# Norms after the two feed-forwards: statistics by token from the sums' banks, the residual added there by TensorE, normed pieces turned back

## The chip, the cores and the metric

The kernel runs on one core of one Trainium2 chip. The metric is the device time of one execution in microseconds (us); three runs of the kernel before are given. PE is TensorE, PEld its weight loads, DVE is VectorE, ACT is ScalarE, POOL is GpSimd and SP is SyncE, which here only issues DMAs.

## The reference

The model is two blocks of two layers each on 256 tokens of width 1024, in float32. The change touches only the second block, and in it only the residual and layer norm behind each feed-forward:

```
DEEPNORM_ALPHA = (2 * DEPTH) ** 0.25        # DEPTH = 2
def layer_norm(x, g, b):
    mu = jnp.mean(xf, -1, keepdims=True)
    var = jnp.mean(jnp.square(xf - mu), -1, keepdims=True)
    y = (xf - mu) * lax.rsqrt(var + LN_EPS) * g + b
def conv_ffn(x, w_up, conv_w, conv_b, w_down):        # w_up 1024 x 5632, w_down 2816 x 1024
    h = causal_depthwise_conv(x @ w_up, conv_w) + conv_b
    gate, val = jnp.split(h, 2, axis=-1)
    return (jax.nn.silu(gate) * val) @ w_down
for layer in range(DEPTH):                            # the second block
    mix = even_mixer(...) if layer % 2 == 0 else odd_mixer(...)
    h = layer_norm(DEEPNORM_ALPHA * h + mix, ln_g[layer, 0], ln_b[layer, 0])
    ffn = conv_ffn(h, ...)
    h = layer_norm(DEEPNORM_ALPHA * h + ffn, ln_g[layer, 1], ln_b[layer, 1])
return h
```

## The kernel before

The running activation `X` lies in SBUF by feature: 128 partitions hold 128 features, and eight chunks of 256 columns hold the tokens. Weights stream as 842 tiles of 128x1024 through a ring of four slots (SP, L447). Every product of the large weights is made in three passes of split float32: ACT writes the high part of each half tile (`split_high`, L1200), DVE the low part (`split_low`, L2241), and PE multiplies low by high, high by low and high by high (L537 to L539, or L579 to L581). Each engine has its own program, written out by hand in the order of issue; semaphores order the engines against each other. The `h_high` and `h_low` operands of a product are the split of its input, made in pairs of chunks (L1309, L1913, L1917), and a product's first tile waits for each pair.

`conv_ffn` first makes the 44 chunks of the up projection (`split_linear`), with the convolution and the gate on ACT and DVE. Then `down` runs 22 tiles: `split_sums` holds a pair of token blocks of the gated activation still and streams the weight rows, so that the sums lie by token in the four banks of `PA`: bank `t * 2 + b` has token block `t` (128 tokens) and features `512 b` to `512 b + 511`. A filler matmul (`busy`, L601) stands between the up and the down part, and others in the norms.

Behind the last down tile comes this chain. ACT and DVE copy `PA` to `TMP` (L1270, L1848; `TMP` is a part of `BIG`, and that name stands in the rows). PE turns 16 blocks of 128x128 back to features in `PB` (`turn_sums`, L589). DVE adds the residual chunk by chunk (`add_chunk`, L1841). PE sums `X` over the features with a matrix of 1/1024 (L642), DVE subtracts the mean (L1936), ACT squares (L1261), PE sums the squares (L628), ACT takes the root (L1265), DVE its reciprocal on 128x256 (L1893) and scales (L1898), and ACT applies gain and shift (`affine`, L1303). After the first feed-forward the odd mixer's product `odd_in` follows, and between its first and its second tile eight small gate matmuls (L1094). After the second, SP stores the four pairs of `X` (L482).

## Time and profile before

| | us |
|---|---|
| median of 3 runs (lowest to highest) | 3028.68 (3025.34 to 3029.73) |
| profiled execution, its own time | 3028.78 |
| its span from first to last instruction | 3027.1 |
| PE busy in it | 2913.8 (96%) |
| DVE busy | 2272.9 (75%) |
| ACT busy | 1646.3 (54%) |

The profiled execution lies 0.10 us above the median, and 1.68 us of its time lie outside the span. A busy PE is not a PE at its peak: matmuls overlap, so one that takes 0.40 us starts 0.23 us after the one ahead of it. The mean granted clock of TensorE was 0.991 of full.

### The profile page before, as it was taken

The page shows a single profiled execution, that of the slowest core. Times are in us where ns is not written, and L with a number is a line of the kernel's source. Part 1 is how long each engine was busy: PE and PEld are TensorE (multiplying, and loading weights), DVE is VectorE, ACT ScalarE, POOL GpSimd, SP SyncE. Part 2 cuts the span into 40 slices and gives each one's busy share as a digit, 9 for nine tenths or more (in the row PEclk, how much of TensorE's full clock was granted, in tenths as well). Part 3 has the DMA queues.
Part 4 walks back from the last instruction along what each step waited for, and adds up shares of the span by engine and source line. Part 5 has one row for each costly group of instructions (what it writes and reads, how often), then busy time and mean ns, then how long its engine had stood idle before and what let it go on. Part 6 is the DMA issues. An engine that isn't in the chain of part 4 may idle for free.

```text
span 3027.1 us, 58260 instructions
## 1 busy us (share of the span) xinstructions
PE 2913.8 (96%) x19784; PEld 2655.7 (88%) x19784; DVE 2272.9 (75%) x4828; ACT 1646.3 (54%) x3387; POOL 62.0 (2%) x112
## 2 busy tenths in 40 slices
PE   7988999999999999999999999999999999999998
PEld 6988999999887778899999988888898889797896
DVE  5586598888779984759888877777585678765786
ACT  2323557778544443655777854444554258463574
POOL 2000000000001100000000000000000000000000
PEclk9999999999999999999999999999999999999999
DMA  9611454444478853445444455555442155432453
GB/s 367 260 54 63 167 186 158 154 161 140 165 265 307 309 194 119 139 167 186 157 153 161 140 173 187 187 188 188 142 140 70 43 172 173 160 126 84 152 175 118
DMA packets 137688, 503.07 MB, mean 166 GB/s; under 512 B 15312, under 2 KB 15440, under 8 KB 137264
## 3 DMA queue, kind: packets, MB, share of 16 engines
q1 hardware_dynamic: 122544, 445.63, 43.5%
q0 software_dynamic: 14976, 55.19, 5.1%
q8 instruction: 107, 1.75, 0.2%
q14 instruction: 61, 0.50, 0.1%
HBM read 498.65 MB, written 2.10 MB: 165 GB/s over the span
## 4 chain that ended last, share of the span: by engine, by line
PE 82%; DVE 6%; ACT 3%; issue 2%; DVEq 0%; ACTq 0%
PE PB L537 14%; PE PB L538 14%; PE PB L539 13%; PE PA L580 9%; PE PA L581 9%; PE PA L579 9%; PE PA L773 4%; PE PB L527 2%; DVE w_low L2241 2%; PE PA L985 1%; DVE BIG L2267 1%; PE PA L1159 1%; PE PA L628 1%; ACT w_high L1200 1%; PE PB L985 1%
## 5 line engine op out<-in xcount | busy, mean ns | idle before, releaser
L1200 ACT ACTIVATE w_high<-ring 128x512 fp32r<-128x512 f32 x1596 | 992.1, 630 | 886.6 <-PE PA L581 466.3
L2241 DVE TENSOR_TENSOR w_low<-ring,w_high 128x512 fp32r<-128x512 f32 x1596 | 1084.2, 691 | 454.8 <-ACT w_high L1200 439.4
L537 PE MATMUL PB<-h_high,w_low 128*128 128x256 f32 x3984 | 1139.4, 286 | 20.7 <-DVE h_low L1917 10.5
L538 PE MATMUL PB<-h_low,w_high 128*128 128x256 f32 x3984 | 1124.6, 282 | 0.0
L539 PE MATMUL PB<-h_high,w_high 128*128 128x256 f32 x3984 | 1122.0, 282 | 0.0
L537 PEld LDWEIGHTS PB<-h_high,w_low 128*128 128x128 f32 x3984 | 760.3, 191 | 34.8 <-issue 17.1
L538 PEld LDWEIGHTS PB<-h_low,w_high 128*128 128x128 f32 x3984 | 753.9, 189 | 0.4 <-issue 0.2
L539 PEld LDWEIGHTS PB<-h_high,w_high 128*128 128x128 f32 x3984 | 753.2, 189 | 0.0
L579 PE MATMUL PA<-w_low,a_high 128*128 128x512 f32 x1200 | 470.4, 392 | 7.8 <-DVE a_low L2250 7.0
L580 PE MATMUL PA<-w_high,a_low 128*128 128x512 f32 x1200 | 476.3, 397 | 0.0
L581 PE MATMUL PA<-w_high,a_high 128*128 128x512 f32 x1200 | 474.0, 395 | 0.0
L579 PEld LDWEIGHTS PA<-w_low,a_high 128*128 128x128 f32 x1200 | 225.4, 188 | 74.0 <-DVE a_low L2250 9.8
L580 PEld LDWEIGHTS PA<-w_high,a_low 128*128 128x128 f32 x1200 | 224.9, 187 | 53.0
L581 PEld LDWEIGHTS PA<-w_high,a_high 128*128 128x128 f32 x1200 | 225.2, 188 | 49.3
L773 PE MATMUL PA<-onehot_b,onehot_a 128*128 128x128 f32 x1024 | 137.6, 277 | 2.9 <-issue 2.6
L2250 DVE TENSOR_TENSOR a_low<-BIG,a_high 128x256 fp32r<-128x256 f32 x300 | 127.6, 425 | 10.3
L773 PEld LDWEIGHTS PA<-onehot_b,onehot_a 128*128 128x128 f32 x1024 | 124.8, 191 | 6.7 <-issue 3.3
L1860 DVE SCALAR_TENSOR_TENSOR BIG<-BIG,coef 128x1024 f32<-128x1024 f32 (+1 forms) x80 | 102.5, 1281 | 13.6 <-DMA BIG<-ada 12.3
L1414 ACT ACTIVATE onehot_a<-inv,slots 128x128 f32<-128x128 f32 x256 | 111.0, 481 | 0.0
L2267 DVE SCALAR_TENSOR_TENSOR BIG<-PB,par,BIG 128x255 f32 (+3 forms) x176 | 84.5, 480 | 14.8 <-DVE BIG L2267 14.5
L1409 ACT ACTIVATE inv<-con,slots 128x128 f32<-128x128 f32 x256 | 88.5, 393 | 4.8 <-PE PA L773 3.2
L2181 DVE TENSOR_TENSOR onehot_b<-con,slots 128x512 f32<-128x512 f32 x128 | 87.7, 685 | 0.0
(341 smaller groups left out, 2604.6 us busy)
## 6 DMA issues: line engine op xcount, KB each, us to landing
ring<-tiles SPq DMA_DIRECT2D x842, 512.0 KB, 3.3
BIG<-ada POOLq DMA_DIRECT2D x96, 512.0 KB, 6.9
BIG<-skew POOLq DMA_DIRECT2D x4, 512.0 KB, 4.5
X<-x SPq DMA_DIRECT2D x1, 1024.0 KB, 5.8
skew<-BIG POOLq DMA_DIRECT2D x1, 1024.0 KB, 6.6
out<-X SPq DMA_DIRECT2D x4, 256.0 KB, 2.1
con<-consts SPq DMA_DIRECT2D x1, 911.0 KB, 8.7
BIG<-masks POOLq DMA_DIRECT2D x1, 768.0 KB, 7.9
```

Source lines behind the costliest of these rows:

```text
L537: mm(dst, lhs_l, high, start=start, stop=False, skip_group_check=True)
L538: mm(dst, lhs_h, low, start=False, stop=False, skip_group_check=True)
L539: return mm(dst, lhs_h, high, start=False, stop=stop, skip_group_check=True)
L579: mm(dst, high[:, own], w_l, start=first, stop=False, skip_group_check=True)
L580: mm(dst, low[:, own], w_h, start=False, stop=False, skip_group_check=True)
L581: ins = mm(dst, high[:, own], w_h, start=False, stop=last, skip_group_check=True)
L773: ins = mm(PA[:, (g % 4 * 4 + i) * P:(g % 4 * 4 + i + 1) * P], onehot_a[:, i * P:(i + 1) * P], onehot_b[:, i * P:(i + 1) * P], start=True, ...
L1200: fn(tile_half(w_high, s, b), ring[:, at:at + HALF], ACT.Identity).then_inc(sem("high_ready"), 1)
L1414: ins = fn(onehot_a[:, i * P:(i + 1) * P], inv[:, i * P:(i + 1) * P], ACT.Relu, scale=slots[:, 3 * T + tok:3 * T + tok + 1], bias=slots[:, ...
L2241: tt(tile_half(w_low, s, b), ring[:, at:at + HALF], tile_half(w_high, s, b).bitcast(F32), ALU.subtract).then_inc(sem("low_ready"), 1)
L2250: tt(pair(a_low, j), a, pair(a_high, j).bitcast(F32), ALU.subtract)\
L2267: stt(dst, product_slot(q0 + j)[:, 0:T - sh], wt[tap][:, bass.ds(it * 4 + j, 1)], dst, ALU.mult, ALU.add).then_inc((taken, sem("conv_step" ...
```

## The change

The down sums no longer start from zero. `add_residual` first writes alpha times `X` into the four banks of `PA`, by token: 16 float32 matmuls that hold a 128x128 block of `X` still and stream a new constant, alpha times the identity; the filler between up and down goes. After the last down tile the layer norm is taken by token: DVE's `bn_stats` reads each bank as soon as its last matmul is done, `bn_aggr` makes mean and variance of each token, ACT takes two roots of one column, DVE makes a scale and a shift for each token. ACT then writes the normed first half of the features to `TMP`, DVE the second, PE turns the pieces back, and ACT applies gain and shift from `PB` straight into `X`. Two filler matmuls stand ahead of the turning. Three semaphores are merged into two names of the same kind (`exponent_ready`, `exponential_ready`), which moves nothing.

```diff
-    ("tri", P), ("strict", P), ("pairs", PAIR_LEVELS * P), ("eps", 2),
+    ("tri", P), ("strict", P), ("pairs", PAIR_LEVELS * P), ("eps", 2), ("alpha", P),
...
+        TOK_STATS, TOK_MEANS = inv[:, 0:TT * 12], inv[:, 24:24 + TT * 2]
+        TOK_ROOTS, TOK_SCALES, TOK_SHIFTS = inv[:, 28:28 + TT], inv[:, 30:30 + TT], inv[:, 32:32 + TT]
+        def token_piece(ap, t, b):
+            return ap[:, t * D + b * HALF:t * D + (b + 1) * HALF]
+        def turned(m):
+            at = (product_at["odd_in"][0] + m // 2) % 4 * 512 + m % 2 * T
+            return PB[:, at:at + T]
...
+            def add_residual():
+                for t in range(TT):
+                    for m in range(DC):
+                        mm(PA[:, t * D + m * P:t * D + (m + 1) * P], X[:, m * T + t * P:m * T + (t + 1) * P],
+                           c("alpha"), start=m % 4 == 0, stop=False, skip_group_check=True)
...
                         ins = mm(dst, high[:, own], w_h, start=False, stop=last, skip_group_check=True)
+                        if tokens and t == 0:
+                            ins.then_inc(sem("first_tokens"), 1)
...
+            def turn_normed():
+                for b, normed in enumerate(("sums_copied", "normed_by_dve")):
+                    for t in range(TT):
+                        pe.wait_ge(sem(normed), w.up(sem(normed)))
+                        for m in range(4 * b, 4 * b + 4):
+                            ins = nc.tensor.transpose(turned(m)[:, t * P:(t + 1) * P],
+                                                      TMP[:, t * D + m * P:t * D + (m + 1) * P], ident)
+                            if t and m % 2:
+                                ins.then_inc(sem("sums_turned"), 1)
...
                 def down(j, it=0):
-                    split_sums(c0 + j, s0 + 2 * FC + j, it, 4, j == 0, j == FC - 1)
-                busy(1, PA[:, 1024:1024 + HALF])
+                    split_sums(c0 + j, s0 + 2 * FC + j, it, 4, False, j == FC - 1, j == FC - 1)
+                add_residual()
...
-                turn_sums()
+                busy(2, PB[:, 0:HALF])
+                turn_normed()
...
+            def token_norm(name, run=None):                       # on ACT
+                if run is not None:
+                    split_high(run, 0)
+                for t in range(TT):
+                    act.wait_ge(sem("mean_ready"), w.up(sem("mean_ready")))
+                    fn(TOK_ROOTS[:, t:t + 1], TOK_MEANS[:, 2 * t + 1:2 * t + 2], ACT.Sqrt,
+                       bias=c("eps", 1, 1)).then_inc(sem("root_ready"), 1)
+                for t in range(TT):
+                    act.wait_ge(sem("scaled"), w.up(sem("scaled")))
+                    fn(token_piece(TMP, t, 0), token_piece(PA, t, 0), ACT.Identity, scale=TOK_SCALES[:, t:t + 1],
+                       bias=TOK_SHIFTS[:, t:t + 1]).then_inc(sem("sums_copied"), 1)
+            def turned_affine(i, name, run=None):
+                for m in range(DC):
+                    if m % 2 == 0:
+                        act.wait_ge(sem("sums_turned"), SUMS.index(name) * (DC // 2) + m // 2 + 1)
+                    ins = fn(X[:, m * T:(m + 1) * T], turned(m), ACT.Identity,
+                             scale=p("ln_g", i * DC + m, 1), bias=p("ln_b", i * DC + m, 1))
+                    if m % 2:
+                        ins.then_inc(sem("x_out"), 1)
+                        w.up(sem("x_out"))
+                        if run is not None and m // 2 >= HIGH_BY_ACT:
+                            act.wait_ge(sem("x_out"), (i + 1) * (DC // 2) + m // 2 + 1)
+                            fn(two(h_high, m // 2), two(X, m // 2), ACT.Identity).then_inc(sem("pair_high"), 1)
+                if run is not None:
+                    split_high(run, 1)
...
+            def token_norm(i, run=None):                          # on DVE
...
+                def scaled(t):
+                    dve.wait_ge(sem("root_ready"), w.up(sem("root_ready")))
+                    v.reciprocal(TOK_SCALES[:, t:t + 1], TOK_ROOTS[:, t:t + 1]).then_inc(done, 1)
+                    settled()
+                    stt(TOK_SHIFTS[:, t:t + 1], TOK_MEANS[:, 2 * t:2 * t + 1], -1.0, TOK_SCALES[:, t:t + 1],
+                        ALU.mult, ALU.mult).then_inc(sem("scaled"), 1)
+                def normed(t):
+                    dve.wait_ge(sem("scaled"), w.up(sem("scaled")))
+                    ts(token_piece(TMP, t, 1), token_piece(PA, t, 1), TOK_SCALES[:, t:t + 1],
+                       TOK_SHIFTS[:, t:t + 1], ALU.mult, ALU.add).then_inc(sem("normed_by_dve"), 1)
+                if run is not None:
+                    split_low(run, 0)
...
+                        v.bn_stats(TOK_STATS[:, at:at + 6], token_piece(PA, t, b)).then_inc(done, 1)
...
+                            v.bn_aggr(TOK_MEANS[:, 2 * t:2 * t + 2], TOK_STATS[:, t * 12:(t + 1) * 12])\
+                                .then_inc(sem("mean_ready"), 1)
...
+                for t in range(TT):
+                    scaled(t)
+                for t in range(TT):
+                    normed(t)
+                if run is not None:
+                    for m in range(DC // 2):
+                        split_fresh(X, "x_out", m)
+                    split_low(run, 1)
...
-        "eps": np.tile([1e-6, 1e-5], (P, 1)),
+        "eps": np.tile([1e-6, 1e-5], (P, 1)), "alpha": ALPHA * eye,
```

On PE, between the last up tile and the first down tile of each feed-forward, there stood before one filler matmul (L601):

```order
L539 MATMUL PB<-h_high,w_high 128x256
L183 REGISTER_ALU
L183 COMPARE_AND_BRANCH
L601 MATMUL PA<-con 128x512
L579 MATMUL PA<-w_low,a_high 128x512
```

Now 16 matmuls of `X` with the constant stand there (L585), and the first down tile (L597) is queued behind them:

```order
L550 MATMUL PB<-h_high,w_high 128x256
L183 REGISTER_ALU
L183 COMPARE_AND_BRANCH
L585 MATMUL PA<-con,X 128x128 x16
L597 MATMUL PA<-w_low,a_high 128x512
```

On DVE, behind the first feed-forward's last split of the gated activation, there stood before the copy of the sums, the residual, two tiles' low parts, the mean, the reciprocal of 256 columns and the scaling:

```order
L1848 COPY BIG<-PA 128x1024
L1841 SCALAR_TENSOR_TENSOR X<-X,PB 128x256 x8
L2241 TENSOR_TENSOR w_low<-ring,w_high 128x512 x2
L1936 TENSOR_TENSOR X<-X,PA 128x512 x4
L2241 TENSOR_TENSOR w_low<-ring,w_high 128x512 x2
L1893 RECIPROCAL inv<-inv 128x256
L1898 TENSOR_TENSOR X<-X,inv 128x512 x3
L1913 CAST h_high<-X 128x512
L1917 TENSOR_TENSOR h_low<-X,h_high 128x512
```

Now the low part of `odd_in`'s first tile comes ahead of the statistics, that of its second tile behind the split of `X`, and between them only four pieces of 512 columns are read from `PA` and two written:

```order
L2350 TENSOR_TENSOR w_low<-ring,w_high 128x512 x2
L2036 BN_STATS inv<-PA 128x6 x3
L2040 BN_AGGR inv<-inv 128x2
L2036 BN_STATS inv<-PA 128x6
L2040 BN_AGGR inv<-inv 128x2
L2015 RECIPROCAL inv<-inv 128x1
L2017 SCALAR_TENSOR_TENSOR inv<-inv 128x1
L2015 RECIPROCAL inv<-inv 128x1
L2017 SCALAR_TENSOR_TENSOR inv<-inv 128x1
L2022 TENSOR_SCALAR BIG<-PA,inv 128x512 x2
L1975 CAST h_high<-X 128x512
L1979 TENSOR_TENSOR h_low<-X,h_high 128x512
```

On ACT, behind the last feed-forward, there are now one table load, two roots of one column, two pieces and the eight chunks; the four squares and the copy of 1024 columns are gone:

```order
L1349 ACT_TABLE_LOAD
L1349 ACTIVATE inv<-inv,con 128x1 x2
L1353 ACTIVATE BIG<-PA,inv 128x512 x2
L1361 ACTIVATE X<-PB,par 128x256 x8
L207 UNCONDITIONAL_BRANCH
```

The table load stands ahead of the first root's wait and behind the last `split_high`, where it has nothing to wait for.

## Rows read from the trace of the kernel before

**Rows 1.** The page: shares of the chain that ended last, by engine

```profile
PE 82%; DVE 6%; ACT 3%; issue 2%; DVEq 0%; ACTq 0%
```

**Rows 2.** Stretches: length, busy (x count) of PE, PEld, DVE, ACT, POOL, PEclk, DMA, GB/s

```profile
2650.40:2655.90 5.50, 4.87 (x25) 4.66 (x26) 3.25 (x7) 2.86 (x6) 0.00 (x0) 0.69 0.00 0
...
2944.00:3005.50 61.50, 61.23 (x263) 48.85 (x261) 42.70 (x86) 25.29 (x40) 0.00 (x0) 1.00 0.43 146
3005.50:3024.60 19.10, 13.43 (x58) 9.52 (x58) 10.70 (x18) 9.22 (x15) 0.00 (x0) 0.99 0.08 29
```

**Rows 3.** Timeline behind the second feed-forward: start, duration, engine, line [idle before <-releaser]

```profile
3005.09 0.40 PE L581 MATMUL PA<-w_high,a_high 128*128 128x512 f32 x1
3005.53 1.23 DVE L1848 COPY BIG<-PA 128x1024 f32<-128x1024 f32 x1 [3.55 <-PE PA L581]
3006.80 1.97 PE L589 MATMUL PB<-con,BIG 128*128 128x128 f32 x16 [1.32 <-DVE BIG L1848]
3007.50 2.74 DVE L1841 SCALAR_TENSOR_TENSOR X<-X,PB 128x256 f32<-128x256 f32 x8 [0.75 <-PE PB L589]
...
3018.07 1.75 DVE L1893 RECIPROCAL inv<-inv 128x256 f32<-128x256 f32 x1 [3.26 <-ACT inv L1265]
...
3020.59 4.04 ACT L1303 ACTIVATE X<-X,par 128x256 f32<-128x256 f32 x8 [2.62 <-DVE X L1898]
...
3021.70 3.28 SPq L482 DMA_DIRECT2D out<-X  x4
```

**Rows 4.** Timeline around the first feed-forward's end and the odd mixer's start

```profile
2627.39 0.63 ACT L1200 ACTIVATE w_high<-ring 128x512 fp32r<-128x512 f32 x1 [0.76 <-PE PA L581]
...
2628.05 0.69 DVE L2241 TENSOR_TENSOR w_low<-ring,w_high 128x512 fp32r<-128x512 f32 x1 [0.70 <-ACT w_high L1200]
...
2632.53 0.40 PE L581 MATMUL PA<-w_high,a_high 128*128 128x512 f32 x1
...
2650.38 0.36 PE L537 MATMUL PB<-h_high,w_low 128*128 128x256 f32 x1 [1.26 <-DVE h_low L1917]
...
2652.38 0.41 PE L539 MATMUL PB<-h_high,w_high 128*128 128x256 f32 x1
...
2655.70 3.61 PE L1094 MATMUL PA<-X,SM 128*128 128x256 f32 x16
```

**Rows 5.** Timeline of PE between the first feed-forward's up and down parts

```profile
2568.17 1.02 PE L601 MATMUL PA<-con 128*128 128x512 f32 x2
...
2570.83 0.50 PE L579 MATMUL PA<-w_low,a_high 128*128 128x512 f32 x1 [1.64 <-DVE a_low L2250]
...
2573.49 0.40 PE L581 MATMUL PA<-w_high,a_high 128*128 128x512 f32 x1
...
2574.15 0.49 PE L579 MATMUL PA<-w_low,a_high 128*128 128x512 f32 x1 [0.26 <-DVE a_low L2250]
```

**Rows 6.** Groups by shape: count | busy us, mean ns of one | idle before

```profile
L1451 ACT ACTIVATE BIG<-PB,par 128x256 f32 x80 | 43.9, 548 | 0.0
L1614 ACT ACTIVATE BIG<-PB 128x256 f32<-128x256 f32 x24 | 9.2, 383 | 29.5 <-PE PB L539 29.5
L1261 ACT ACTIVATE BIG<-PA 128x512 f32<-128x512 f32 x6 | 3.6, 597 | 10.9 <-PE PA L732 10.9
L1791 DVE TENSOR_SCALAR BIG<-PB,par 128x256 f32<-128x256 f32 x8 | 4.4, 544 | 12.7 <-PE PB L527 12.7
```

**Rows 7.** Timeline: one-column steps and a reduction of 512 columns

```profile
2658.63 0.20 ACT L1619 ACTIVATE stat<-stat 128x2 f32<-128x2 f32 x1
...
2659.06 0.15 DVE L2534 TENSOR_SCALAR stat<-stat 128x1 f32<-128x1 f32 x1
...
2687.85 0.69 DVE L2508 TENSOR_REDUCE stat<-BIG 128x2 f32<-128x512 f32 x1
```

**Rows 8.** Timeline: 16 float32 matmuls of 128 columns in the first 40 us

```profile
22.38 3.65 PEld L616 LDWEIGHTS PB<-coef,BIG 128*128 128x128 f32 x32 [3.00 <-DMA BIG<-ada]
```

**Rows 9.** DMA issue of the constants: count, KB each, us from issue to landing

```profile
con<-consts SPq DMA_DIRECT2D x1, 911.0 KB, 8.7
```

More of the change, by code:

```diff
@@ L568, in split_linear, with split_sums @@
                 spans(pe, body, (first, n if last is None else last))
-            def split_sums(j, k, it, step, first=False, last=False):
+            def add_residual():
[3 more added lines that the diff above has]
+                           c("alpha"), start=m % 4 == 0, stop=False, skip_group_check=True)
+            def split_sums(j, k, it, step, first=False, last=False, tokens=False):
                 pe.wait_ge(sem("gated_ready"), it * 4 + (j + 1))
@@ L1617, in odd_mixer @@
                     if j == 0:
-                        act.wait_ge(sem("lam_sums"), w.up(sem("lam_sums")))
-                        fn(stat[:, 8:10], stat[:, 6:8], ACT.Exp).then_inc(sem("lam_exp"), 1)
+                        act.wait_ge(sem("exponent_ready"), w.up(sem("exponent_ready")))
+                        fn(stat[:, 8:10], stat[:, 6:8], ACT.Exp).then_inc(sem("exponential_ready"), 1)
                         act.wait_ge(sem("gate_psum"), w.up(sem("gate_psum")))
@@ L1654, in _ @@
             fn(coef[:, 0:DC], p("c", 0, DC), ACT.Silu).then_inc(sem("cond_ready"), 1)
-            act.wait_ge(sem("lb_shifted"), w.up(sem("lb_shifted")))
-            fn(coef[:, 40:48], coef[:, 40:48], ACT.Exp).then_inc(sem("lb_exp"), 1)
+            act.wait_ge(sem("exponent_ready"), w.up(sem("exponent_ready")))
+            fn(coef[:, 40:48], coef[:, 40:48], ACT.Exp).then_inc(sem("exponential_ready"), 1)
             act.wait_ge(sem("x_loaded"), w.up(sem("x_loaded"), 16))
@@ L1741, in _ @@
             conv_ffn(0)
-            layer_norm("down0", "odd_in")
-            norm_affine(1)
+            token_norm("down0", "odd_in")
+            turned_affine(1, "down0", "odd_in")
             odd_mixer()
@@ L1747, in _ @@
             conv_ffn(1)
-            layer_norm("down1")
-            norm_affine(3, split=False)
+            token_norm("down1")
+            turned_affine(3, "down1")
         @block.vector
@@ L1899, in scale @@
                         .then_inc(sem("scaled"), 1)
+                w.up(sem("scaled"), DC // 2)
                 if name is not None:
@@ L1942, in layer_norm, with settled @@
                 scale(X, "x_out" if run is not None else None)
+            def token_norm(i, run=None):
+                done = sem("dve_step")
+                def settled():
+                    dve.wait_ge(done, w.up(done))
+                def scaled(t):
[10 more added lines that the diff above has]
+                    split_low(run, 0)
+                r0, n = STREAM_AT[f"down{i}"]
+                s1 = SPLIT_AT[f"up{i}"][0] + 3 * FC
+                for b in range(2):
+                    for t in range(TT):
+                        if t == 0:
+                            dve.wait_ge(sem("first_tokens"), w.up(sem("first_tokens")))
+                        else:
+                            dve.wait_ge(*((sem("mid_tile"), s1), (tile_done, r0 + n))[b])
+                        at = (t * 2 + b) * 6
+                        v.bn_stats(TOK_STATS[:, at:at + 6], token_piece(PA, t, b)).then_inc(done, 1)
+                        w.up(done)
+                        if b:
+                            dve.wait_ge(done, w.value(done))
+                            v.bn_aggr(TOK_MEANS[:, 2 * t:2 * t + 2], TOK_STATS[:, t * 12:(t + 1) * 12])\
+                                .then_inc(sem("mean_ready"), 1)
+                            w.up(sem("mean_ready"))
+                            dve.wait_ge(sem("mean_ready"), w.value(sem("mean_ready")))
+                for t in range(TT):
+                    scaled(t)
+                for t in range(TT):
+                    normed(t)
[3 more added lines that the diff above has]
+                    split_low(run, 1)
             def inverse_heads(n):
@@ L2290, in conv_ffn @@
                 spans(dve, tile, (2, FC + 2, 2 * FC, 2 * FC + 2, 3 * FC))
-                add_sums(f"down{i}")
+                token_norm(i, ("odd_in", None)[i])
             def even_mixer():
@@ L2495, in odd_mixer @@
                 dve.wait_ge(sem("dve_step"), w.up(sem("dve_step")))
-                v.tensor_reduce(stat[:, 6:8], lv[:, :, 0, :], AX.X, ALU.add).then_inc(sem("lam_sums"), 1)
+                v.tensor_reduce(stat[:, 6:8], lv[:, :, 0, :], AX.X, ALU.add).then_inc(sem("exponent_ready"), 1)
                 def biased(n):
@@ L2700, in _ @@
             conv_ffn(0)
-            layer_norm(1, "down0", "odd_in")
             odd_mixer()
```

11 lines of the change are left out of this document (5 added, 6 removed).

## Prediction

> **What bounds the kernel now.** I read four views in this order. The page's chain of work that ended last puts 82% of the span on PE [rows 1], so a saving counts only where PE waits or where the last stage ends. The stretches then show two kinds of time: in the second down part PE is busy 61.23 us of 61.50 with 263 matmuls, one each 0.23 us, at the full granted clock, while behind it 19.10 us pass with DVE busy 10.70 and ACT 9.22: no engine is full, it is one chain [rows 2]. The timeline of that stretch shows it link by link, and the one at the first feed-forward and the one between up and down show the two other places that the change touches [rows 3 to 5].
>
> I call E the end of the last down matmul: 3005.09 + 0.40 = 3005.49 in the second feed-forward, 2632.53 + 0.40 = 2632.93 in the first [rows 3, 4]. Behind the second, the last chunk of `X` is ready at 3020.59 + 4.04 = 3024.63, so E + 19.14 [rows 3]. Behind the first, `odd_in` starts at 2650.38 = E + 17.45, and its first tile is followed by the gate matmuls at 2655.70 = E + 22.77 [rows 4]. From there PE goes on alone, so this second number is the one that passes to the end.
>
> **The change, part by part.**
>
> *Prices.* A reduction of 512 columns on DVE takes 0.69 us [rows 7], a copy of 1024 columns from PSUM 1.23 [rows 3], so 256 more columns cost (1.23 - 0.69) / 2 = 0.27. `bn_stats` stands nowhere in the trace. From below: it can't matter much under 0.69, since the first two banks are done before E. From above: the slowest row per column is the reciprocal, 1.75 us for 256 [rows 3], so 3.50 for 512. I take 0.69, the row of the same kind (one operand read once, a small result), and keep 1.4 (twice over the data) for the range. A one-column step costs 0.15 on DVE and 0.20 on ACT [rows 7], with 0.04 between steps. A piece of 512 from PSUM on ACT costs 0.60 plus two pointer operands; those cost 0.548 - 0.383 = 0.165 on 256 columns [rows 6], so 0.76. On DVE, 256 columns with two pointers take 0.544 [rows 6], 512 then 0.81. The eight chunks stay at 4.04 / 8 = 0.505 each [rows 3]; between 0.46 and 0.55 the tail moves by 0.4.
>
> *Behind the second feed-forward.* The four banks end at E - 2.09, - 1.39, - 0.70 and 0, three matmuls of 0.23 apart. DVE is free, so three `bn_stats` run from E - 2.05 to + 0.04, `bn_aggr` to 0.25, the fourth `bn_stats` 0.29 to 0.98, its `bn_aggr` to 1.17. The root of the second tokens ends on ACT at 1.41; meanwhile DVE makes the first tokens' scale and shift, ready at 1.6, and the second's at 2.0. ACT writes its pieces 1.62 to 2.4 and to 3.1, DVE 2.0 to 2.8 and to 3.65. The two fillers take PE to E + 2.0 at most (one takes 1.02 [rows 5]), ahead of the first piece. The turning of four blocks takes 4 x 0.12 (16 in 1.97), and the reader follows 0.45 behind the second block's start, as DVE's first add follows the fourth by about as much [rows 3]. The last pieces of the first features are turned from 3.15, so ACT's chunks start at 3.6. The second features are turned by 4.5, ahead of ACT. End: 3.6 + 4.04 = E + 7.65 against 19.14: **- 11.5 us**. The stores follow the chunks as before (issued over 3.28 us from the first pair on [rows 3]) and stay 2.5 us behind the last.
>
> *Behind the first feed-forward.* Here the low part of `odd_in`'s first tile is queued on DVE ahead of the statistics. Its second half needs the last but one down tile off PE (E - 2.79), then 0.63 on ACT and 0.69 on DVE [rows 4], so DVE is free at E - 1.37 and everything is 0.7 late against the other tail: chunks start at E + 4.35. The first pair is out at 5.4; DVE casts and subtracts it (0.42 and 0.69), and PE starts at E + 6.65 against 17.45. ACT does six chunks (to 7.4), a high part (0.63), two chunks, a high part (to 9.8), DVE the last low part to 10.5. A pair is six matmuls: 0.70 us at full clock. In the row at 2652.38 a matmul of 256 columns takes 0.41 instead of 0.28 and the stretch from 2650.40 has a granted clock of 0.69 [rows 2, 4]: part of the tile ran at 1.2 GHz, after gaps in PE's work. I take the same here: PE finishes pairs at 7.9, 9.2, 10.5 and 11.8. Gate matmuls at E + 11.8 against 22.77: **- 10.9 us**. The high part of the second tile has moved behind all this on ACT and its low part on DVE, ready by E + 12: the gate matmuls (3.6 us [rows 4]) cover it by 3 us, and with it the loads that SP issues on each low part. Without that cover it would cost up to 1.4.
>
> *Between up and down, twice.* 16 float32 matmuls of 128 columns took 3.65 us [rows 8]. They start at 2568.17, where the filler did, so the first down tile starts at 2571.83 instead of 2570.83: 1.0 late. It then ends at 2573.73 + 1.0, where the second tile started at 2574.15, held by the split of its activation on DVE [rows 5]: that slack of 0.4 is taken up, and **+ 0.6 each, + 1.2** goes on, since the down part is PE's alone. In the second feed-forward it is the same picture.
>
> *At the start.* The constants grow by 64 KB on 911, which landed in 8.7 us [rows 9], and all engines wait for them: 0 to + 0.6, I take **+ 0.3**. `bn` results, `TMP` and the merged semaphores cost nothing of their own.
>
> Sum against the profiled execution: 3028.78 - 11.5 - 10.9 + 1.2 + 0.3 = **3007.9**. The median of the runs is 0.1 lower than that execution; I say 3007.8.
>
> **A rule that speaks against it.** The rows show the granted clock at 0.99 through the stretch of [rows 2] that holds 16 turnings, fillers and sums; they don't show turnings with nothing dense behind them. The Trainium skill, "TensorE: Matmul & The Clock Gate", Part 4 (PE-mode transpose), says that the full clock "doesn't engage" for transposes. By that rule the turned pieces would not keep PE warm ahead of `odd_in`; the result would be the first rival below, by the row alone the sum above.
>
> **Rivals.**
> 1. *A cold start of the odd mixer.* Five fillers and sixteen summing matmuls stood ahead of `odd_in`; now only two fillers and the turnings, with gaps. If the slow level lasts through the tile and the gate matmuls, these take 7.2 instead of 3.6 us, less what the next tiles' ACT and DVE work hides. The slow stretch before was there at 2652.38 and gone at 2655.70, where 16 gate records take 3.61, so some 3 us [rows 4]; one that lasts through the gate matmuls too loses 1.5 to 3.6 more, I take 2.7: 3010.5. For it: PE idles from about E + 5 to 6.65, then 0.5 between pairs. Chance 0.22.
> 2. *`bn_stats` reads twice.* At 1.4 us the four of them end 0.7 x 4 = 2.8 later in each tail, since they stand one behind the other: 3007.8 + 5.6 = 3013.4. Against it: a reduction of 512 columns goes once over the data. Chance 0.10.
> 3. *The other side: `bn_stats` as slow per column as the reciprocal.* 3.50 each adds (3.50 - 0.69) x 4 = 11.2 per tail, 22.4 in all: 3030.2, slower than before. It decides from 3.3 us each. Nothing but that one row speaks for it. Chance 0.02.
> 4. *It is worth only one tail.* The odd mixer waits for something other than `X`, say its tables on POOL. Against: PE's first matmul there is released by `h_low` [rows 4]. 3007.8 + 10.9 = 3018.7, chance 0.02.
>
> **How the numbers follow.** The forecast has 0.64, the rivals the rest. The likeliest case has its own range of 3005.5 to 3010 (clock at full throughout - 0.6, chunks at 0.46 - 0.7, constants - 0.3; gaps of 0.1 on some ten links + 1 to 2). The range over the cases takes in rival 1 and most of rival 2: 3004.0 to 3013.5. What a measurement of this kernel can tell from no change is about 0.2%, 6 us; faster by more 0.96, within 0.02, slower 0.02.
>
> **What would show it.** In the changed kernel's timeline: `BN_STATS` at 0.69 us, three of them before E + 0.1; ACT's first chunk at E + 3.6 behind the second feed-forward and E + 4.35 behind the first; the last chunk's end at E + 7.65; the gate matmuls at E + 11.8; the 16 residual matmuls in 3.65 us and a second down tile that no longer waits. It would be wrong if a `BN_STATS` takes over 1.2 us, if the granted clock is low beyond `odd_in`'s first tile, or if ACT's chunks, and not PE or DVE, start later than the pieces allow.

## The result, and the profile after

| | before | after |
|---|---|---|
| median (lowest to highest), us | 3028.45 (3025.34 to 3029.73) | 3002.09 (3001.84 to 3006.80) |
| profiled execution, its span, us | 3028.78, 3027.1 | 3006.80, 3005.1 |
| time after by time before, all executions | | 0.9919, 95% interval 0.9906 to 0.9932 |

The change saves 26.4 us by the medians of four executions each. The forecast was 3007.8 with a range of 3004.0 to 3013.5, so the result is 1.9 us under the range. The profiled execution of the changed kernel took 3006.80, 22.0 less than the profiled one before, where the sum said 20.9. The other three took 3002.26, 3001.91 and 3001.84. Four executions are few: the interval of the ratio reaches up to 0.9932, and 0.9932 of 3028.45 is 3007.9, so this measurement misses the stated range and doesn't rule out the forecast's ratio of 0.9931 (3007.8 to 3028.68). So there are two questions: did the steps go as worked out, and where do 4.9 us between executions of one kernel come from?

The timeline of the changed kernel behind the second feed-forward answers to [rows 3]:

```profile
2993.09 2.09 DVE L2036 BATCH_NORM_STATS2 inv<-PA 128x6 f32<-128x512 f32 x3 [1.46 <-PE PA L599]
...
2994.74 0.40 PE L599 MATMUL PA<-w_high,a_high 128*128 128x512 f32 x1
...
2994.98 1.88 PE L632 MATMUL PB<-con 128*128 128x512 f32 x4
2995.21 0.21 DVE L2040 BATCH_NORM_AGGREGATE inv<-inv 128x2 f32<-128x12 f32 x1
...
2995.45 0.70 DVE L2036 BATCH_NORM_STATS2 inv<-PA 128x6 f32<-128x512 f32 x1
...
2996.43 0.29 ACT L1349 ACTIVATE inv<-inv,con 128x1 f32<-128x1 f32 x1 [0.68 <-DVE inv L2040]
...
2996.82 1.45 ACT L1353 ACTIVATE BIG<-PA,inv 128x512 f32<-128x512 f32 x2
...
2997.03 1.52 DVE L2022 TENSOR_SCALAR BIG<-PA,inv 128x512 f32<-128x512 f32 x2
...
2997.66 2.20 PE L610 MATMUL PB<-con,BIG 128*128 128x128 f32 x16 [0.80 <-ACT BIG L1353]
...
2998.80 3.76 ACT L1361 ACTIVATE X<-PB,par 128x256 f32<-128x256 f32 x8 [0.53 <-PE PB L610]
2999.85 3.07 SPq L493 DMA_DIRECT2D out<-X  x4
```

E is 2994.74 + 0.40 = 2995.14. The three first statistics end at 2995.18, E + 0.04. The chunks start at E + 3.66 and end at 3002.56, E + 7.42, where 19.14 stood before. One statistic takes 0.70, a piece 0.73 on ACT and 0.76 on DVE.

The same timeline behind the first feed-forward answers to [rows 4], and the first stretch below to [rows 2]; the second is one of the half-clock stretches in the odd mixer behind it (length, busy (x count) of PE, PEld, DVE, ACT, POOL, granted clock, DMA share, GB/s):

```profile
2632.76 0.39 PE L599 MATMUL PA<-w_high,a_high 128*128 128x512 f32 x1
...
2637.19 2.85 ACT L1361 ACTIVATE X<-PB,par 128x256 f32<-128x256 f32 x6 [0.53 <-PE PB L610]
...
2639.54 0.36 PE L548 MATMUL PB<-h_high,w_low 128*128 128x256 f32 x1 [1.30 <-DVE h_low L1979]
...
2639.74 0.28 PE L549 MATMUL PB<-h_low,w_high 128*128 128x256 f32 x1
...
2643.12 0.38 PE L548 MATMUL PB<-h_high,w_low 128*128 128x256 f32 x1 [0.54 <-DVE h_low L1979]
...
2643.94 3.62 PE L1126 MATMUL PA<-X,SM 128*128 128x256 f32 x16
```

```profile
2631.00:2645.00 14.00, 10.79 (x59) 7.94 (x58) 10.89 (x23) 10.28 (x21) 0.00 (x0) 1.00 0.16 59
2730.90:2737.70 6.80, 6.64 (x35) 4.72 (x36) 2.52 (x5) 0.01 (x1) 0.00 (x0) 0.50 0.01 1
```

E is 2632.76 + 0.39 = 2633.15, the chunks start at E + 4.04, `odd_in` at E + 6.39, its last pair at E + 9.97, behind DVE's last low part, and the gate matmuls at E + 10.79 (22.77 before). The granted clock is 1.00 through this tail: a matmul of 256 columns takes 0.28, not the 0.41 of [rows 4].

Between up and down, against [rows 5], and the constants, against [rows 9]:

```profile
2568.11 3.74 PE L585 MATMUL PA<-con,X 128*128 128x128 f32 x32
2571.60 0.48 PE L597 MATMUL PA<-w_low,a_high 128*128 128x512 f32 x1
```

```profile
con<-consts SPq DMA_DIRECT2D x1, 975.0 KB, 9.0
```

### The stages of five executions

With the timelines of every profiled execution I cut the span at six places: the last matmul of the first up part, E of both tails, the first gate matmul, the last matmul of the second up part and the last chunk's end. The table is worked out from these rows; "lowest" is the lowest profiled execution of the changed kernel (e9 below), the last two are e14 and e13. All in us.

| stage | before | after | after, lowest | filled before | filled after |
|---|---|---|---|---|---|
| start to end of the first up part | 2568.33 | 2568.27 | 2563.89 | 2564.07 | 2563.73 |
| residual or filler, down part, to E | 64.60 | 64.88 | 64.89 | 64.59 | 64.89 |
| E to the gate matmuls | 22.77 | 10.79 | 10.77 | 22.06 | 10.77 |
| odd mixer and second up part | 285.19 | 286.33 | 283.60 | 280.64 | 280.63 |
| residual or filler, down part, to E | 64.60 | 64.87 | 64.87 | 64.60 | 64.89 |
| E to the last chunk | 19.14 | 7.42 | 7.42 | 19.13 | 7.41 |
| to the end of the span | 2.46 | 2.55 | 2.57 | 2.47 | 2.55 |
| half-clock stretches in the odd mixer (3.4 us each) | 3 | 4 | 2 | 0 | 0 |

Where the clock is the same, the stages that the change touches repeat to 0.03 us between executions of a kernel. What differs between executions is the first row and the odd mixer. One stretch before lies outside the odd mixer's row, at the end of the first tail (2652), and makes it 22.77 instead of 22.06. The filled kernels are explained with e13 and e14; their fillers stand in the first tail of e14 too.

### The profile page after: what moved, and what is told of

It is laid out like the page before. It is cut to its first block, busy times and chain, and to the rows that moved or that the text cites. A ratio compares the mean times of both kernels' runs of the same rounds, so it can differ in the third digit from the quotient of the medians.

```text
span 3005.1 us, 58212 instructions
## 1 busy us (share of the span) xinstructions
PE 2899.8 (96%) x19768; PEld 2647.4 (88%) x19768; DVE 2261.7 (75%) x4816; ACT 1642.2 (55%) x3383; POOL 61.9 (2%) x112
## 4 chain that ended last, share of the span: by engine, by line
PE 85%; DVE 3%; ACT 3%; issue 1%; ACTq 0%; DVEq 0%
PE PB L548 15%; PE PB L549 15%; PE PB L550 14%; PE PA L598 9%; PE PA L599 9%; PE PA L597 9%; PE PA L804 4%; PE PB L538 2%; PE PA L1017 1%; PE PA L1191 1%; DVE w_low L2350 1%; PE PA L659 1%; ACT w_high L1230 1%; PE PA L690 1%; PE PB L1017 1%
## 5 line engine op out<-in xcount | busy, mean ns | idle before, releaser
L597 PE MATMUL PA<-w_low,a_high 128*128 128x512 f32 x1200 | 470.2, 392 | 3.9 <-DVE a_low L2359 3.2
L597 PEld LDWEIGHTS PA<-w_low,a_high 128*128 128x128 f32 x1200 | 225.4, 188 | 67.8 <-issue 6.7
```

The costliest lines, as they stand in the source:

```text
L597: mm(dst, high[:, own], w_l, start=first, stop=False, skip_group_check=True)
```

## The experiments

A filler is one `busy` matmul of 128x512.

### The changed kernel again: e1, e5, e9, e15

No edit. 

> The changed kernel again, nothing edited. Theory A (the tails gave 22 us as in the profiled run of 3006.80; the rest of the difference is that executions differ in how many stretches of TensorE run at the half clock): single times lie at two or more levels, near 3001.9 and near 3006.8, and a profile of the shorter kind shows one to three fewer half-clock stretches at places that the change does not touch, with the tails as before at E + 7.4 and E + 10.8. Theory B (the tails or the matmuls behind the first tail are themselves shorter in the usual execution): a shorter profile shows the first tail's gate matmuls or the last chunk earlier than these by over 1 us.

Measured: median 3006.80 (3002.60 to 3008.54), ratio 0.9929 (0.9915 to 0.9943). The profiled execution was a long one (3008.47), with its last chunk at E + 7.43 and its gate matmuls at E + 10.78.

> One more look at the changed kernel, unedited, for its profile. Theory A (the 4.9 us between its short and its long executions are half-clock stretches of TensorE): if the time is near 3002, stretches at 1287, 2301 and 2400 us or one or two of those between 2730 and 2795 us are missing and the first tail's gate matmuls stand at E + 10.8, the last chunk at E + 7.4, as in the long execution; if it is near 3007 or 3008, all are there. Theory B (tails shorter): in a short execution a tail is over 1 us shorter.

Measured: 3006.41, a long one again. Tails E + 7.41 and E + 10.78.

> The changed kernel, unedited, beside the three that follow. By the sum of my steps 20.9 us under before, by its profiled executions 22; the single executions spread over 3002 to 3008.5 as before, with the low ones those without the half-clock stretches at 303, 1287, 2301 and 2400 us.

Measured: median 3005.82 (2999.70 to 3007.84), ratio 0.9928 (0.9914 to 0.9941), and now the profiled execution is a short one, 2999.70. Two groups of twelve matmuls of the even mixer, its head sums and the spreading of the heads' roots, in the timeline of the profiled execution of the section above:

```profile
2299.52 4.23 PE L682 MATMUL PA<-BIG,con 128*128 128x256 f32 x12 [3.30 <-ACT BIG L1291]
...
2399.43 4.54 PE L690 MATMUL PA<-inv,con 128*128 128x256 f32 x12 [2.33 <-DVE inv L2055]
```

and in e9, with three of its stretches:

```profile
2298.27 2.83 PE L682 MATMUL PA<-BIG,con 128*128 128x256 f32 x12 [3.31 <-ACT BIG L1291]
...
2396.51 2.86 PE L690 MATMUL PA<-inv,con 128*128 128x256 f32 x12 [2.33 <-DVE inv L2055]
```

```profile
1285.00:1292.00 7.00, 5.84 (x46) 5.43 (x46) 5.32 (x10) 4.75 (x9) 0.00 (x0) 1.00 0.15 39
2298.00:2304.00 6.00, 5.73 (x39) 5.45 (x40) 1.29 (x2) 2.84 (x6) 0.00 (x0) 1.00 0.44 156
2396.00:2402.00 6.00, 4.72 (x25) 3.80 (x25) 4.32 (x7) 1.89 (x3) 0.00 (x0) 1.00 0.00 1
```

The waits ahead of the two groups are the same to 0.01 us (3.30 and 2.33), the matmuls behind them are not: 4.23 against 2.83, 4.54 against 2.86. The same three places in the long execution:

```profile
1287.00:1290.40 3.40, 3.29 (x15) 3.29 (x16) 2.47 (x5) 2.08 (x4) 0.00 (x0) 0.50 0.02 5
2300.80:2304.20 3.40, 3.40 (x12) 2.74 (x11) 0.69 (x2) 1.26 (x1) 0.00 (x0) 0.50 0.44 152
2399.80:2403.20 3.40, 3.40 (x10) 2.64 (x9) 0.94 (x2) 0.63 (x1) 0.00 (x0) 0.50 0.01 2
```

Clock 0.50 is 1.2 GHz, 1.00 is 2.4. The short execution is 1.25 us ahead at 2299.52, 2.92 at 2399.43 and 4.38 at the end of the first up part: 1.7 us for the second of these stretches, 1.5 for the third. The odd mixer is 2.73 shorter with two stretches fewer. These two rows of the table make the whole difference of the spans (4.38 + 2.73 = 7.11). The tails are the same, so theory B falls. The stretch at 303, which the expectation named too, is still there in e9.

No profile was kept of the three short executions of the first measurement, but each execution's mean granted clock is on record. Of the 20 of the unedited changed kernel, the six at 3002.6 or less, these three among them, have 0.993 to 0.995, and the fourteen at 3005.56 or more have 0.991 or 0.992. That fits theory A.

> The changed kernel, unedited, on the same chip, for the spread: two groups near 3001 and near 3006.5.

Measured: median 3007.23 (3005.56 to 3008.22), ratio 0.9932 (0.9918 to 0.9945): no low one in five.

### Parts of the change: e2, e3, e4

e2 takes the second feed-forward alone, e3 the first; in the other one the old filler, `turn_sums`, `add_sums` and `layer_norm` stand (e3 has `(0,)` in the first line):

```diff
+BY_TOKEN = (1,)
...
-                add_residual()
+                if i in BY_TOKEN:
+                    add_residual()
+                else:
+                    busy(1, PA[:, 1024:1024 + HALF])
```

> The change in the second feed-forward alone, the first keeps the old tail. Sum of my steps: -11.7 for the last tail, +0.5 between up and down, +0.3 for the constants: 10.9 less than before, 3017.5 against a median before of 3028.4. If the unexplained 4.9 us of the usual execution belong to the second half of the change or to the start (the constants), this run shows them here: 3012.6. If they come with the first tail, it stays at 3017.5.

Measured: 3016.38 (3014.08 to 3019.44), ratio 0.9961 (0.9948 to 0.9975), 10.4 under before. In the profile: E + 7.41 for the last chunk, E + 22.78 for the gate matmuls.

> The change in the first feed-forward alone. Sum of my steps: -12.0 for the tail up to the gate matmuls, +0.5 between up and down, +0.3 for the constants, +1 for one more half-clock stretch in the odd mixer as in the profiled run: 10.2 less than before, 3018.2. If the unexplained 4.9 us come with the first tail or the odd mixer behind it, 3013.3.

Measured: 3015.35 (3012.00 to 3019.89), ratio 0.9963 (0.9950 to 0.9977), 11.5 under before. In the profile: gate matmuls at E + 10.78, last chunk at E + 19.13. Each was forecast near what it gave (10.9 and 10.2) and not 4.9 more. The halves add to 21.9; neither holds a hidden 4.9.

e4 is the kernel before with the longer constants:

```diff
-    ("tri", P), ("strict", P), ("pairs", PAIR_LEVELS * P), ("eps", 2),
+    ("tri", P), ("strict", P), ("pairs", PAIR_LEVELS * P), ("eps", 2), ("alpha", P),
```

> The kernel before, but the constants are loaded with the 64 KB more that the change needs, and nothing uses them. The later landing of the constants costs 0.3 us: 3028.7. If the shift of the start changes which stretches of TensorE fall to the half clock (theory A), the median moves by 1 to 5 us either way, with the tails unchanged; if the 4.9 us belong to the tails (theory B), it stays within 0.5 us of before.

Measured: 3026.29 (3023.23 to 3030.46, 11 executions), ratio 0.9998 (0.9989 to 1.0007). The constants landed 0.1 later than in [rows 9]'s execution, and the median did not move by what can be told. But the profiled execution was a short one, a span of 3021.5 against 3027.1 of the kernel before, and it lacks the half-clock stretches at 1287, 2301 and 2400 and two of three in the odd mixer (that stage: 282.19 against 285.19). So the kernel before has a spread of the same kind, at the same places.

### Single costs: e8, e12, e6, e7

e8 leaves the residual out, so that the sums start from zero again:

```diff
-                    split_sums(c0 + j, s0 + 2 * FC + j, it, 4, False, j == FC - 1, j == FC - 1)
+                    split_sums(c0 + j, s0 + 2 * FC + j, it, 4, j == 0, j == FC - 1, j == FC - 1)
...
-                add_residual()
+                busy(1, PA[:, 1024:1024 + HALF])
```

> The changed kernel with the residual left out (the norms are then taken of the feed-forward's sum alone); the old filler matmul stands again ahead of the down part and the first term starts the sum. My step priced the 16 residual matmuls at 0.6 us for each of the two places, the profile of the changed kernel showed 0.35 to 0.45: 0.8 us less than the changed kernel (1.2 by my price). If the 16 matmuls are hidden behind the wait for the first pieces, no change.

Measured: 3002.70 (3000.84 to 3005.50), ratio 0.9919 (0.9906 to 0.9933). Its timeline has the picture of [rows 5] again:

```profile
2567.33 1.02 PE L632 MATMUL PA<-con 128*128 128x512 f32 x2
2569.99 0.50 PE L597 MATMUL PA<-w_low,a_high 128*128 128x512 f32 x1 [1.64 <-DVE a_low L2359]
...
2573.31 0.49 PE L597 MATMUL PA<-w_low,a_high 128*128 128x512 f32 x1 [0.27 <-DVE a_low L2359]
```

From the up part's end to E it takes 64.59 and 64.60, as before; against the 64.88 and 64.87 of the changed kernel the residual's price is 0.29 and 0.27, 0.56 in all. The median can't show that: half-clock stretches move it by more, and it lies 3.7 under the one unedited execution on this chip, not 0.8.

e12 takes every statistic twice:

```diff
                         v.bn_stats(TOK_STATS[:, at:at + 6], token_piece(PA, t, b)).then_inc(done, 1)
+                        dve.wait_ge(done, w.up(done))
+                        v.bn_stats(TOK_STATS[:, at:at + 6], token_piece(PA, t, b)).then_inc(done, 1)
```

> Each bank's statistics are taken twice, one behind the other. My step: three of the four lie beside the last nine matmuls and only the last one behind E. Doubled they are six of 0.70 + 0.04 from E - 2.05, so the third bank's end at E + 2.4 in place of E + 0.1, and the last bank's pair takes 0.74 more: last chunk E + 10.5, the first tail's gate matmuls E + 13.8, 6.2 us in all, 3013 against 3006.8. If the statistics were the hidden bound in full (nothing beside the matmuls), the doubled cost would be 4 x 0.74 = 3.0 for each tail too, but with the first three pairs starting only at E; the rows tell it.

Measured: 3011.53 (3006.31 to 3014.26), 5.7 over e9 on the same chip; last chunk E + 10.57 (10.5 expected), gate matmuls E + 14.14 (13.8 expected).

```profile
2996.97 0.70 DVE L2038 BATCH_NORM_STATS2 inv<-PA 128x6 f32<-128x512 f32 x1
...
3000.88 3.40 PE L610 MATMUL PB<-con,BIG 128*128 128x128 f32 x16 [3.53 <-ACT BIG L1353]
3002.45 3.75 ACT L1361 ACTIVATE X<-PB,par 128x256 f32<-128x256 f32 x8 [0.96 <-PE PB L610]
```

E is 2995.63, the third bank's second statistic ends at 2997.67, E + 2.04, where the single ones ended at E + 0.04: three more statistics are 2.1 us of DVE, and 2.0 of it now shows, since the cover of the last nine matmuls was already used up. With 0.73 for the last bank and 0.4 for the turnings, which fall into a half-clock stretch (3.40 for 2.20), it makes the 3.15 by which the last tail is longer; the first is longer by 3.35. Undoubled, the first three of the four end with the last matmul and cost next to nothing.

e6 takes out the two fillers ahead of the turnings:

```diff
-                busy(2, PB[:, 0:HALF])
                 turn_normed()
```

> The changed kernel without the two filler matmuls ahead of the turnings. They end at E + 1.7, the first normed piece comes at E + 2.5, so nothing waits for them: 3006.8 (as its unedited kernel on this chip) within 1 us. If the fillers are what keeps TensorE at its full clock through the tail, a stretch at the half clock appears in the first tail: by the same stretch's rows elsewhere (0.7 to 1.6 us each) 3007.5 to 3008.4, or no change of the sum if it only moves there from the odd mixer.

Measured: 3006.34 (3004.01 to 3008.25), ratio 0.9935 (0.9921 to 0.9948): no difference in the time. The turnings of the first tail and of the last, and the first tail's stretch:

```profile
2632.68 3.67 PE L610 MATMUL PB<-con,BIG 128*128 128x128 f32 x16 [2.89 <-ACT BIG L1352]
```

```profile
2994.87 2.20 PE L610 MATMUL PB<-con,BIG 128*128 128x128 f32 x16 [2.51 <-ACT BIG L1352]
```

```profile
2629.80:2641.00 11.20, 7.79 (x40) 7.21 (x41) 7.97 (x18) 8.10 (x16) 0.00 (x0) 0.70 0.12 46
```

Without the fillers PE waits 2.89 us in the first tail, the clock falls, the same turnings take 3.67, and `odd_in`'s first pair and half of its second run at half clock. In the last tail the clock did not fall: after a wait of 2.51 us the turnings take 2.20, as with fillers. In the first it costs only 0.42 (gate matmuls at E + 11.20), and all of that is in the turnings: from `odd_in`'s start to the gate matmuls pass 4.39 us, as with fillers (4.40), since ACT and DVE set the pace of the pairs. The last pair ran at the full clock in both. The odd mixer takes 286.47, so nothing is given back there.

e7 shares the last tail's chunks: ACT (the first lines) writes the even chunks of `X`, DVE the odd ones behind them:

```diff
+                if run is None:
+                    for m in range(0, DC, 2):
...
+                done_by_act = 8
+                for m in range(1, DC, 2):
+                    dve.wait_ge(sem("sums_copied"), done_by_act + m // 2 + 1)
+                    ts(X[:, m * T:(m + 1) * T], turned(m), p("ln_g", 3 * DC + m, 1), p("ln_b", 3 * DC + m, 1),
+                       ALU.mult, ALU.add).then_inc(sem("x_out"), 1)
```

> The last tail's eight chunks of X are shared: ACT writes the even ones, VectorE the odd ones behind them, so that the pitch of a pair is bound by the turnings (the last at E + 4.7) and not by ACT's 0.47 each. Even chunks 4 and 6 by about E + 5.9, the last odd one E + 6.2 against E + 7.4: 1.2 us less than the changed kernel. If VectorE and ACT hinder each other in PSUM, less than 0.5.

Measured: 3002.98 (2999.11 to 3007.46), ratio 0.9923 (0.9909 to 0.9936). The profiled execution was a short one.

```profile
2994.92 1.93 ACT L1361 ACTIVATE X<-PB,par 128x256 f32<-128x256 f32 x4 [0.53 <-PE PB L610]
2995.52 1.91 DVE L2062 TENSOR_SCALAR X<-PB,par 128x256 f32<-128x256 f32 x4 [0.84 <-ACT X L1361]
2996.09 1.81 SPq L493 DMA_DIRECT2D out<-X  x4
```

The last chunk is at E + 6.18 (E is 2991.25), 1.24 earlier, as worked out. But the span ends 3.26 behind it and not 2.55: the four stores are issued over 1.81 us instead of 3.07, and their median from issue to landing is 2.6 us instead of 2.2. The gain is 0.53. A saving in front of transfers that are pushed together is partly paid there; my step had left the stores out.

### Fillers in waits that the change doesn't touch: e10, e11, e13, e14

> The changed kernel with filler matmuls in four waits of TensorE that the change does not touch: six ahead of the first head sums of the even mixer (wait 3.3 us, 2296 to 2299.5), four ahead of each spreading of the heads' roots (2.3 us, 2397 and 2757), seven in place of five behind a layer norm's squares (1284). They end before what TensorE waits for. Theory A (the half-clock stretches behind these waits are the spread): the stretches at 1287, 2301, 2400 and 2761 are gone in every execution, so the time is 0.7 + 1.6 + 1.5 + 1.6 = 5.4 us under the long executions of the changed kernel, 3001.5, and the spread narrows from 6.7 to some 3 us. Theory B (the spread is in the tails or comes from the transfers): same times and same spread as the unedited kernel.

Measured: 3007.01 (3003.52 to 3008.09), ratio 0.9931 (0.9917 to 0.9944): no gain, theory A's 3001.5 missed. The timeline shows why:

```profile
2295.80 5.31 PE L632 MATMUL PA<-con 128*128 128x512 f32 x12
...
2300.95 2.75 PE L682 MATMUL PA<-BIG,con 128*128 128x256 f32 x12
```

One filler is two rows and takes 0.9 us, not 0.45. Six of them reached 1.7 us past the wait, four at the spreading 0.9. The sums behind them do run at the full clock (2.75), and a new half-clock stretch came at 2430. Fillers that reach too far cost time while the stretches that they remove give it back. Two things were mixed, and the run decides nothing.

> The fillers of the kernel before this one, and the last tail's chunks shared by ACT and VectorE (measured there alone: last chunk at E + 6.2 for E + 7.4). The two savings lie in different places and add: 1.2 us under the filled kernel, 3000.3.

Measured: 3006.21 (3003.10 to 3006.78), last chunk E + 6.16, end of the span 3.27 behind it: by the stages 0.56 less than e10, as in e7, not 1.2.

e13 has fillers sized to the waits in the changed kernel, e14 the same ones in the kernel before. They stand ahead of the even mixer's head sums, ahead of `spread_heads` in both mixers, around a norm's sums of squares and in the odd mixer's decay attention:

```diff
+                    if i == 0:
+                        busy(3, PA[:, 1536:2048])
...
+                busy(2, PA[:, 1024:1536])
...
+                busy(1, PB[:, 0:HALF])
                 mean_squares(norm_bank(name, 0))
-                busy(5, PB[:, 0:HALF])
+                busy(6, PB[:, 0:HALF])
...
-                        busy(1, PA[:, 1536:2048])
+                        busy(1 if n else 3, PA[:, 1536:2048])
```

> The changed kernel with fillers of the right size: a filler takes 0.9 us (8 rows in 3.60), so three go into the wait of 3.3 ahead of the head sums at 2296, two into each wait of 2.3 ahead of the spreading, one more behind a layer norm's squares and one ahead of them (waits of 1.3 and 1.9), two more in the first step of the odd mixer's decay attention (3.05). None reaches over what TensorE waits for. Theory A: the half-clock stretches at 1287, 2301, 2400, 2731, 2761 and 2792 us are gone in every execution, none comes in their place at 2430; the lowest unedited execution (2999.7) had two of the last three at 1.4 each, so 2997 to 3000, median 2998.5, all executions below 3001. Theory B (fillers and clock have nothing to do with the spread): the same two groups as the unedited kernel, 3001 and 3006.5.

Measured: 2997.67 (2996.39 to 2999.04, 4 executions), ratio 0.9901 (0.9886 to 0.9917), beside 0.9932 for the unedited kernel on the same chip: 9.6 us less than its median there, and every one of the four below the lowest of the 20 unedited executions (2999.70).

```profile
2290.00:2304.00 14.00, 13.36 (x87) 11.27 (x87) 3.88 (x6) 10.90 (x14) 0.00 (x0) 1.00 0.35 114
2390.00:2402.00 12.00, 9.71 (x44) 6.98 (x44) 6.63 (x8) 4.50 (x7) 0.00 (x0) 1.00 0.00 1
...
2639.40:2920.10 280.70, 275.01 (x2161) 253.38 (x2160) 200.24 (x390) 174.42 (x338) 0.00 (x0) 1.00 0.43 140
```

The granted clock is 1.00 at both places and through the whole odd mixer and second up part, which take 280.63. Against the long profiled execution (3006.80 to 2996.56, 10.24) the table puts 4.54 on the first row and 5.70 on the odd mixer, the two rows where the stretches were. Theory A stands: where the stretches are gone, so is the time. That the spread goes with them isn't shown by this run, since its four executions spread by 2.7 us and the five unedited ones on the same chip (e15) also by 2.7.

> The same fillers in the kernel before. Its lowest executions are 3023.2 to 3023.7, with one stretch of 1.5 in the odd mixer: median 3022, all below 3024.5. The difference of the two filled kernels is then the change alone, without moved stretches: 11.72 + 11.98 for the tails, less 2 x 0.27 for the residual and 0.1 for the constants, 23.1 us. If the moved stretch of the odd mixer is not what took 1.2 of it, 21.9.

Measured: 3019.37 (3018.23 to 3021.91, 9 executions), ratio 0.9975 (0.9965 to 0.9985). The expectation was 3022, so the fillers gave more than was counted. All nine lie below the lowest of 50 unedited executions (3023.46), and they spread by 3.7 us, where the 13 unedited ones on this chip spread by 5.6. One stretch that they were meant for, at 1287, is still there in the profiled execution. Its stretch over the same stage:

```profile
2650.70:2931.40 280.70, 275.04 (x2159) 253.39 (x2158) 199.36 (x387) 174.36 (x338) 0.00 (x0) 1.00 0.42 138
```

The stage is the same as in e13 to 0.01 us. So at the full clock the odd mixer neither gained nor lost by the change. The two filled kernels differ by 21.7 in their medians and by 22.7 in their profiled spans; by the stages of the change alone it is 11.29 + 11.72 - 0.30 - 0.29 - 0.08 = 22.3. My 23.1 was too high because it took the first tail's 22.77, which holds a half-clock tile of its own; at the full clock, as in e14, it is 22.06.

## Why the prediction was wrong, step by step

**Last tail, E + 19.14 to E + 7.65.** Right: E + 7.42. The statistic at 0.69 (0.70), the pieces at 0.76 and 0.81 (0.73 and 0.76), the chunks' start at 3.6 (3.66) and the chunks at 0.505 (0.47) were as priced. The one-column root took 0.29 instead of 0.20, which moved the first piece by less than 0.1.

**First tail, gate matmuls E + 22.77 to E + 11.8.** The links were right (chunks E + 4.04 for 4.35, `odd_in` E + 6.39 for 6.65), the term too small: 11.98 was gained, where 22.77 - 11.8 is 10.97 (put into the sum as 10.9). Of the 1.01 between E + 11.8 and E + 10.79, DVE's last low part gave 0.58 (ready at E + 9.92, where the prediction had 10.5), and the last pair behind it 0.43: it was priced at half clock, 1.3 us, and took 0.87 at the full one. That all four pairs are paced by PE's clock was wrong: ACT and DVE pace them. In e6 the half clock in the first one and a half pairs cost nothing (4.39 for 4.40). The two fillers did not give this, since in e6 the last pair ran at full without them; what they gave there is 0.42 in the turnings.

**"From there PE goes on alone, so this second number is the one that passes to the end."** Not quite. Of the 11.98 gained, 1.14 was lost in the odd mixer of the profiled pair, which has four half-clock stretches for three. The one that stood at 2652 behind the old tail is gone and another came. I had seen the half clock only where [rows 2, 4] showed it, in the piece of time that I was costing.

**Residual, + 1.2.** A size: + 0.55 (64.88 and 64.87 for 64.60, twice), shown alone by e8. The matmuls delay the first down tile by 0.83, and down tiles that no longer wait for their activation take back 0.55. I had counted 1.0 and 0.4. The delay was priced to the end of the last matmul, but matmuls overlap: the 16 take 3.74, and the next one starts 3.49 behind the first. The 3.65 of [rows 8] is also a row of weight loads (PEld), not of the matmuls themselves.

**Constants, + 0.3.** Landed 0.3 later (9.0 for 8.7 us), but with the longer constants the landing lies anywhere from 8.7 (e13) to 9.6 (e7), and e4 shows nothing in the time that can be told.

**The sum.** By stages 11.98 + 11.72 - 0.28 - 0.27 - 1.14 - 0.09 = 21.9 against the 20.9 of the forecast. The profiled executions differ by 22.0. Part of this nearness is luck: the first tail gave 1.1 and the residual 0.65 more than forecast, and the odd mixer, for which there was no term, took 1.14 back.

**The range.** This is the step that failed. "Sum against the profiled execution" was taken as the kernel's level, with 0.1 us to the median, and "clock at full throughout - 0.6" was all that the clock was given. The terms named for the low side (0.6, 0.7 and 0.3) give 3006.2, the text says 3005.5, and nothing is named for the step down to 3004.0. But one execution of the changed kernel differs from another by up to 8.8 us (2999.70 to 3008.54 in 20 executions, median 3006.15), one of the kernel before by 7.3 (3023.46 to 3030.77 in 50, median 3027.49), through half-clock stretches at places outside the change. Six of the 20 lie at 3002.6 or less, fourteen at 3005.6 or more, and three of those six were among the four of the first measurement. So it was chance of the draw which side of the range's lower end the median fell on: the three later measurements of the same kernel have medians of 3006.80, 3005.82 and 3007.23, all inside the range and within 2 us of the forecast. Over all of them the change is worth 21.3 by the medians and 22.1 by the means. The range should have been widened by the spread between executions, some 4 us down. It was in sight: the three executions on hand spread by 4.4 us (3025.34 to 3029.73), the prediction itself says that a measurement tells no less than 6 us from no change, and the mean granted clock of 0.991 hinted at the cause: 0.009 of 3027 us is 27 us of missing clock, and it was not asked where.

**The rivals.** A start of the odd mixer at half clock did not happen (granted 1.00 from 2631 to 2645). The Trainium skill, "TensorE: Matmul & The Clock Gate", Part 4 (PE-mode transpose), says that the full clock "doesn't engage" for transposes. In this case the turned pieces ran in 2.20 us at the full clock with two fillers ahead of them, in 3.67 (e6, first tail, no fillers) and 3.40 (e12, a wait of 3.53 us behind the fillers) at the half clock, and in 2.20 again in e6's last tail, without fillers; so here the turnings run at whatever clock is granted when they start; that they keep PE at the half clock, as the rule would have it, the trace does not show. The statistics took 0.70 us, not 1.4 or 3.5, and both tails paid.

**What stays open.** Why one execution of the same kernel has the stretches at 1287, 2301 and 2400 and the next has none of them, with waits equal to 0.01 us, isn't settled; of the profiled executions without fillers upstream, those that lack them lack all three. Nor is it known whether the change makes the short form likelier, or why the odd mixer of the changed kernel had four stretches where the kernel before had three. That the fillers keep the clock up in the first tail rests on one profiled execution (e6), whose last tail kept it without them. The stretches in the first 100 us weren't tried; they and the one at 1287 may be what leaves the filled kernels spreads of 2.7 and 3.7 us.

## What to carry to other kernels

A sum over stages can be right to a microsecond and the measured time still miss it by five, where half-clock stretches come and go between executions: list those of the profile before costing anything, count 1.5 us for each (1.4 to 1.7 here), and put those that may come or go into the range. Take more executions than three or four before the lowest or the middle one is called the kernel's time. A chain behind a matmul part is shortened most by what can be read from the banks while the last matmuls run (three of four statistics cost nothing here). Fillers in TensorE's waits, sized by their own row, gave 9.6 us more at six places in the code, nearly half of what the whole change gave.

## What the runs showed of the hardware

At the full clock the odd mixer and the second up part took 280.63 us in e13 and 280.64 in e14, while the same waits on TensorE, of 3.30 and 2.33 us, were followed by a stretch of 3.4 us at 1.2 GHz in one execution of a kernel and not in another. Such a stretch cost (285.19 - 280.64) / 3 = 1.5 us and (286.33 - 280.63) / 4 = 1.4 us each in the odd mixer, 1.5 and 1.7 in the even one (e9). Statistics of a 128x512 bank took 0.70 us, their aggregation 0.21, a root of one column with a bias 0.29. Four stores of 256 KB took a median of 2.2 us from issue to landing when issued over 3.07 us, and 2.6 when issued over 1.81 (e7, e11).
